# Mixture-of-experts stage of a two-layer encoder: steps of 512 inner columns, gathers for two experts at once, down products one step later

## What is computed

```
def _swiglu(h, w1, w3, w2):
    return (jax.nn.silu(h @ w1) * (h @ w3)) @ w2

def _moe(h, router, w1, w3, w2):                  # 8 experts, each token goes to 2
    ...
    top_val, top_idx = lax.top_k(logits, TOP_K)
    gates = jax.nn.softmax(top_val, axis=-1)
    gate_full = jnp.sum(one_hot(top_idx, N_EXPERTS) * gates[..., None], axis=1)
    for e in range(N_EXPERTS):
        out = out + gate_full[:, e:e + 1] * _swiglu(t, w1[e], w3[e], w2[e])
```

## Time and profile before

| | |
|---|---|
| median of 3 executions | 1885.35 us (1885.23 to 1887.1) |
| span of the profiled execution, first to last instruction | 1881.5 us |
| from that span to the median | 3.85 us; the profiled execution's own time is not listed apart from its span |
| PE matmul busy | 1803.4 us, 96% |
| DVE busy | 1344.3 us, 71% |
| ACT busy | 1025.5 us, 55% |
| moved by DMA | 470.67 MB, mean 250 GB/s |
| first up product of the mixture, last scatter | 822.8 us, 1862.6 us |

### The profile page before, as it was taken

The page is one execution under the profiler, slowest core; times in us unless marked ns, Lnnn a source line. Parts: engine busy times, 40 slices in busy tenths (PEclk is TensorE's granted clock), DMA queues, the critical chain, the costliest instruction groups (busy, mean ns, idle before and its releaser), DMA issues.

```text
span 1881.5 us, 31990 instructions
## 1 busy us (share of the span) xinstructions
PE 1803.4 (96%) x12801; PEld 1672.0 (89%) x12801; DVE 1344.3 (71%) x1265; ACT 1025.5 (55%) x1027; POOL 37.4 (2%) x73
## 2 busy tenths in 40 slices
PE   6999999999899999889999999999999999999996
PEld 6788998999788799889989999899899899898995
DVE  4555647444575466578888788888888888887886
ACT  4343443443334334356676667667676676666663
POOL 3000000000000000000000000000000000000000
PEclk9899999999898999979999999999999999999998
DMA  8342544655453345639999999999899999999993
GB/s 250 113 135 91 172 142 155 196 185 179 129 181 117 100 138 162 202 111 359 318 340 360 317 341 364 318 339 362 297 361 318 341 361 316 343 359 318 332 360 126
DMA packets 365521, 470.67 MB, mean 250 GB/s; under 512 B 9666, under 2 KB 331300, under 8 KB 365460
## 3 DMA queue, kind: packets, MB, share of 16 engines
q1 hardware_dynamic: 363124, 462.03, 73.4%
q0 software_dynamic: 2336, 7.78, 1.5%
HBM read 468.60 MB, written 1.06 MB: 250 GB/s over the span
## 4 chain that ended last, share of the span: by engine, by line
PE 86%; DVE 5%; DMA 3%; ACT 3%; issue 2%; SPq 1%; POOL 0%; DVEq 0%; ACTq 0%
PE PS L725 25%; PE PS L726 25%; PE PS L727 25%; DMA R1a_flat<-in_moe_w_dram 3%; PE PS L721 2%; DVE SPL L1613 2%; PE PS L1244 1%; PE PS L917 1%; ACT SPH L1339 1%; PE PS L1015 1%; PE PS L964 1%; PE PS L1003 1%; PE PS L935 0%; DVE st L1820 0%; PE PS L950 0%
## 5 line engine op out<-in xcount | busy, mean ns | idle before, releaser
L725 PE MATMUL PS<-SPH,XGH 128*128 128x256 f32 x1344 | 388.1, 289 | 1.6 <-issue 0.8
L727 PE MATMUL PS<-SPH,XGL 128*128 128x256 f32 x1344 | 381.0, 283 | 0.0
L726 PE MATMUL PS<-SPL,XGH 128*128 128x256 f32 x1344 | 381.0, 283 | 0.0
L1613 DVE TENSOR_TENSOR SPL<-RAW,SPH 128x2048 fp32r<-128x2048 f32 (+2 forms) x105 | 233.9, 2230 | 158.2 <-ACT SPH L1339 157.8
L725 PEld LDWEIGHTS PS<-SPH,XGH 128*128 128x128 f32 x1344 | 258.0, 192 | 8.9 <-issue 2.7
L726 PEld LDWEIGHTS PS<-SPL,XGH 128*128 128x128 f32 x1344 | 258.3, 192 | 5.7 <-issue 1.7
L727 PEld LDWEIGHTS PS<-SPH,XGL 128*128 128x128 f32 x1344 | 258.2, 192 | 0.0
L1339 ACT ACTIVATE SPH<-RAW 128x2048 fp32r<-128x2048 f32 (+2 forms) x105 | 195.4, 1864 | 86.5 <-PE PS L727 77.1
L725 PE MATMUL PS<-XTH,SPH 128*128 128x256 f32 x816 | 235.0, 288 | 2.7 <-DVE XTL L1613 1.4
L726 PE MATMUL PS<-XTL,SPH 128*128 128x256 f32 x816 | 233.0, 286 | 0.0
L727 PE MATMUL PS<-XTH,SPL 128*128 128x256 f32 x816 | 232.8, 285 | 0.0
(11 more groups left out here) (259 smaller groups left out, 4140.5 us busy)
## 6 DMA issues: line engine op xcount, KB each, us to landing
R1a_flat<-in_moe_w_dram SPq DMA_DIRECT2D x56, 1024.0 KB, 7.4
R3a_flat<-in_moe_w_dram SPq DMA_DIRECT2D x56, 1024.0 KB, 9.8
R1b_flat<-in_moe_w_dram SPq DMA_DIRECT2D x56, 1024.0 KB, 7.3
R3b<-in_moe_w_dram SPq DMA_DIRECT2D x56, 1024.0 KB, 9.7
R2a<-in_moe_w_dram SPq DMA_DIRECT2D x56, 1024.0 KB, 5.2
R2b<-in_moe_w_dram SPq DMA_DIRECT2D x56, 1024.0 KB, 5.2
RAW<-in_ffn_w_dram SPq DMA_DIRECT2D x33, 1024.0 KB, 5.2
RAW<-in_w_in_dram SPq DMA_DIRECT2D x28, 1024.0 KB, 5.2
```

Source lines behind the costliest of these rows:

```text
L725: mm(dst, wh, xh, start=start, stop=False)
L726: mm(dst, wh, xl, start=False, stop=False)
L727: return mm(dst, wl, xh, start=False, stop=stop)
L1613: return v.tensor_tensor(dst, src, hi, ALU.subtract)
```

## The change

- A step is a single pass over 512 columns. `up` now makes 128x512 outputs with 512-column products; place "a" and "b" are now the upper and the lower half of the 1024 rows of w1 and w3 (4 blocks each), so a call is 12 products of 512 columns. Silu, `hidden` and `take_turned` work on 512 columns once a step, and four transposes follow each other. The rows of w1 and w3 in HBM are 2 KB long in a transfer, which is still 1 MB.
- `down` of step k is run after the up products of step k+1, also from one expert to the next; the copies to YE and the scatter of expert n are run in the first two steps of expert n+1. Only the last expert has them behind it (`conclude`), where w2's parts go into the free buffers of w1.
- A gather makes 32 products of 256 columns for two experts, once in two experts.
- The low part of w2 has its own room, so that a w2 transfer waits for DVE's split and no longer for PE. The room is that of the attention tables (HK and others) for "b", and GB for "a". So POOL's load of the last gain and bias into GB now waits until all experts are added (`experts_added`), which DVE signals behind the If for further passes.
- The transfers are issued in the order w2a, w2b of step k, then w1a, w1b, w3a, w3b of step k+2.

The diff, cut to its core:

```diff
-    FE = 2 * P
-    STEPS = D_FF_E // (2 * FE)
+    FE = 4 * P
+    STEPS = D_FF_E // FE
+    PAIR = 2
+    GATHERS = N_EXPERTS // PAIR
...
-        S2L = {"a": over("S2al", [P, PIECE], F32R, "QK", PIECE)[:], "b": over("S2bl", [P, PIECE], F32R, "RAW", 0)[:]}
+        GBL = nc.alloc_sbuf_tensor_at("S2al", [P, PIECE], F32R, offset=gb_at)[:]
+        S2L = {"a": GBL, "b": over("S2bl", [P, PIECE], F32R, "HK")[:]}
...
# SP
+            def load2(c, e, k, j):
+                after(sp, lo2[c], k)
...
+                def step(j, following):
+                    load2("a", e, k0 + j, j)
+                    load2("b", e, k0 + j, j)
+                    if following:
+                        load1("a", following[0], k0 + j + 2, following[1])
+                        load1("b", following[0], k0 + j + 2, following[1])
+                        load3("a", following[0], k0 + j + 2, following[1])
+                        load3("b", following[0], k0 + j + 2, following[1])
...
# POOL
+                    if layer == DEPTH - 1 and i == 2:
+                        pool.wait_ge(experts_added, 1)
                     pool.dma_start(GB[:, 0, :], gg[layer].partition_broadcast(P)).then_inc(gb_loaded.sem, 16)
...
# PE
+                    for i, t in enumerate(ts):
+                        mm(dst, XGH[:, t, s], WH[:, i, :], start=(t == 0), stop=False)
+                        mm(dst, XGH[:, t, s], WL[:, i, :], start=False, stop=False)
+                    if fresh_lo is not None:
+                        pe.wait_ge(gather_lo, fresh_lo)
+                    for i, t in enumerate(ts):
+                        last = mm(dst, XGL[:, t, s], WH[:, i, :], start=False, stop=(t == KT - 1))
...
+                    k = k0 + 1
+                    up("a", 0, k, x)
+                    turn_hidden(k - 1)
+                    up("b", 0, k, x)
+                    if earlier:
+                        scatter(n - 1, 0)
+                        scatter(n - 1, 1)
+                        scatter(n - 1, 2)
+                    up("a", 1, k, x)
+                    up("b", 1, k, x)
+                    if earlier:
+                        scatter(n - 1, 3)
+                    down("a", k - 1, n, True, False)
+                    turn_gates(n, earlier)
+                    down("b", k - 1, n, True, False)
+                    def later(k, gather_of=None):
+                        up("a", 0, k, x)
+                        turn_hidden(k - 1)
+                        up("b", 0, k, x)
+                        up("a", 1, k, x)
+                        up("b", 1, k, x)
+                        if gather_of is not None:
+                            pe.wait_ge(gatedT_done, n + 1)
+                            gather(gather_of, 0, k + 1)
+                        down("a", k - 1, n, False, False)
+                        down("b", k - 1, n, False, False)
+                        if gather_of is not None:
+                            gather(gather_of, 1, k + 1)
...
# ACT
+                def period(k, earlier=True, ahead=True):
+                    if earlier:
+                        split2("a", k - 1)
+                        split2("b", k - 1)
+                        take_turned(k - 1)
+                    if ahead:
+                        split1("a", k + 1)
+                    silu(k)
+                    if ahead:
+                        split1("b", k + 1)
+                        split3("a", k + 1)
+                        split3("b", k + 1)
...
# DVE: as on ACT, with hidden(k) behind split1("b", k + 1); the first three
# of an expert's sums behind split1("a", k + 1) of the next one's second step
+                def conclude(n):
+                    k = n * STEPS + (STEPS - 1)
+                    split2("a", k, True)
+                    take_turned(k)
+                    split2("b", k, True)
+                    take_half(n)
+                    for i in range(4):
+                        add_rows(n, i)
...
                 extra_experts(dve, extra, listed[0])
+                dve.sem_inc(experts_added, 1)
```

More of the change, by code:

```diff
@@ L594, in _ @@
             layer_pieces(1)
[L596 to L624, removed]
@@ L1186, in down @@
[L1186 to L1191, removed]
+                    WH, WL = [w[c].rearrange("p (t n) -> p t n", t=KT // 2) for w in (WH, WL)]
+                    dst = PS[:, 2 + 2 * which, :]
+                    ts = range(KT // 2) if c == "a" else range(KT // 2, KT)
@@ L1204, in item, with scatter @@
[L1204 to L1227 removed]
+                def scatter(n, i):
+                    if i == 0:
+                        after(pe, y_act, n + 1)
+                        after(pe, y_dve, n + 1)
+                        pe.wait_ge(gatedT_done, n + 1)
+                    if i == 3:
+                        after(pe, scatter_done, n * 4 + 1)
+                    half, b = i // 2, i % 2
+                    mm(PS[:, SCATTER_BANKS[i], :], GATEDT[:, b * P:(b + 1) * P],
+                       YE[:, half * HALF:(half + 1) * HALF], start=True, stop=True).then_inc(scatter_ready, 1)
@@ L1249, in mixture, with pair @@
+                def pair(p, first=False, final=False, besides=None):
+                    expert(p * PAIR, 0, not first, p)
+                    expert(p * PAIR + 1, 1, True, None, None if final else p + 1, besides)
+                gather(0, 0, 0)
                 pe.wait_ge(rows_lo, 1)
-                gather(0, 1)
-                start(0)
-                with pe.Fori(0, N_EXPERTS - 1) as e:
-                    item(e, True)
+                gather(0, 1, 0)
+                pair(0, first=True)
@@ new lines, in gather, with silu @@
+                def gather(m, width=PAIR * P):
+                    for q, bank in enumerate(GATHER_BANKS):
+                        after(act, gather_ready, m * 8 + (q + 1))
+                        src = PS[:, bank, :].rearrange("p (t s) -> p t s", t=2)
+                        high(XGH[:, 2 * q:2 * q + 2, 0:width], src[:, :, 0:width]).then_inc(gather_hi, 1)
+                def silu(k):
+                    after(act, g_ready["b"], k + 1)
+                    after(act, hidden_done, k)
+                    a.activation(SIL, PS[:, 2, :], ACT.Silu).then_inc(silu_done, 1)
@@ L2113, in mixture, with pair @@
+                def pair(p, first=False, final=False, made=None, besides=None):
+                    e = p * PAIR
+                    expert(e, e, 0, not first,
+                           made=None if final else lambda: one_rows(p + 1, (e + PAIR, e + PAIR + 1), 0))
+                    expert(e + 1, e + 1, 0, True, not final, made, besides)
+                    if not final:
+                        gather(p + 1)
+                one_rows(0, (0, 1), 0)
                 dve.wait_ge(rows_hi, 1)
```

494 lines of the change are left out of this document (270 added, 224 removed).

## The result

The changed kernel takes 1831.8 us (median of 4 executions, 1827.22 to 1833.61), the kernel before in the same measurement 1885.29 us (1884.91 to 1887.1, 4 executions): ratio 0.9714, 95% interval 0.970 to 0.9728. The forecast was 1840.8 us, its range 1835 to 1855. The profiled execution took 1827.22 us, its span 1825.0.

The account below looks back on a forecast made before the run. PE's issue was taken as the bound. 56 x 16.90 + 7 x 4.0 + 11.5 + 6.2 = 992.1 us, 47.7 less; with the tail 44.6 less, span 1836.9, plus 3.85: 1840.8 us, range 1835 to 1855.

Parts of the forecast that it names:

- Up products, transposes, step: Each mixture step: 48 up products of 512 columns, transposes no gain; 17.42 becomes 16.90 us, 29.1 us over 56 steps.
- Gathers: Between experts: seven narrow gathers of 3.5 us become three wide ones of 3.84 us, saving 12.9 us.
- Boundaries: From one expert to the next, without the gather: 4.8 us become 4.0 for each of seven, saving 5.6 us.
- the slow product comes twice (0.8): In the next expert's second step: a scatter split in two places has a slow product behind each piece, 0.8 us.
- I keep 6.2: Mixture's slower first stretch, list of full experts and last half step's waits: 6.2 us before, taken as unchanged.
- The first gather: nothing, -1 to +1: Ahead of the mixture: twice the columns in as many instructions, costed at nothing, bounds -1 to +1 us.
- Tail: After the last expert: GB's transfers are now issued behind the If and land late, +3.1 us, bounds +0.9 to +6.7.
- its 2.88 us of issue: DVE's issue stretch near the end, ending at 1869.82, 3.5 us before GB's use; taken as it stood.
- 2.8 for the slow products, 2.2 for the landing and 1 at the start: Range's low end, 1835 us: no second slow product, GB's transfer landing fastest, first gather 1 us cheaper.
- The lead: In the steps: turned values, w2 and next splits are ready 5 us or more before PE wants them; waits cost nothing.
- Transfers: Each step needs a mean of 372 GB/s; with 2 KB rows at 397 its transfers take 15.5 us, hidden behind PE.
- rival (3): Strided 2 KB rows of w1 and w3 move badly; slower below 309 GB/s, 1966 us at 280; chance 0.02.

Follow-up runs that it names:

- single: The changed kernel with eight gathers of 128 columns, as in the kernel before, everything else kept: 1846.15 us, ratio 0.9801.
- before_no_if: The kernel before without reading the list of full experts and without the If for further passes on SP, PE, ACT and DVE: 1878.52 us.
- again: The changed kernel once more, unedited: 1830.31 us, ratio 0.9713 to the kernel before.
- gb_early: The changed kernel with GB loaded after the last but one step's down product, no longer behind the If: 1827.27 us, ratio 0.9698.
- dve_small: The changed kernel with DVE's small split of the turned values (0.69 us) done twice in each step: 1831.46 us in one execution.

## Why the prediction was right in kind and 9 us too high

By its own steps, all from the mark:

- **Up products, transposes, step.** 56 x 16.90 was forecast, 16.89 measured: 0.6 us less in all. Right. It is read from the starts; no run undoes the 512-column step by itself.
- **Gathers.** 3.84 was forecast, 3.83 measured. Right. The narrow ones, read at 3.5, cost 3.61 in single, which gives back 13.8 us for the 12.9.
- **Boundaries.** I took 4.0 us, and 3.68 was measured: 2.2 us over seven. The failed step is "the slow product comes twice (0.8)". Six of the eight records of the scatter take 1082.25 - 1080.08 = 2.17 us and the slow product behind them 0.63 for 0.23; the other two take 0.45 and theirs 0.64. 2.17 + 0.40 + 0.45 + 0.41 = 3.43, which is what one undivided scatter with one slow product costs in the earlier trace rows: 3.03 + 0.40. Its eight records start 0.43 us apart, and the product behind them is listed 0.03 us after the last one: its lateness is that last record's own time. A scatter is 8 x 0.43 us wherever it is cut, so dividing it is free; I had counted the 0.4 once for each piece.
- **"I keep 6.2."** What is left of the stretch is 986.65 - 56 x 16.89 - 7 x 3.68 - 3 x 3.83 = 3.6 us, 2.6 less. I did name the slower first stretch, and left it at its price; but it was a stretch at half clock, and the change moves the clock's return. Before, 18 of the first up products stood 0.213 us apart where 0.120 is usual, 1.7 us; after, none. The list of full experts, which I said would be hidden, accounts for at most the 0.7 us by which this stretch is shorter in before_no_if. The last few tenths are not accounted for.
- **"The first gather: nothing, -1 to +1."** The first up product comes 1.3 us earlier against the mark (1.5 at like clock there), though one more pair of one-hot rows makes the gather begin 0.4 us later. From the gather's start to the first up product it is 5.91 us after and 7.89 before; single, with the narrow gather, takes 6.85. So 0.9 us of the 2.0 are the clock. Most of the other 1.1 is the 0.83 us of "issue" ahead of the first up product, which stands in all four profiles of the kernel before and its edits and in none of the others; what removed it is not shown. A bound of 1 us on either side was made from instruction counts at one clock.
- **Tail.** +3.1 was forecast and +0.4 measured in the profiled execution, +1.3 in again. The wait for GB is there (2.45 and 3.34 us, gone in gb_early). The failed step is "its 2.88 us of issue" as a constant: 2.1 us of them went, for a reason that I can only narrow to the If and the place of the code. That part is luck: with the gap of dve_small the changed kernel would be near 1834, still just below the range.
- **Span to median.** The profiled execution of before was one of the faster ones by about 2 us, so the 3.85 us were no constant to add to a span. It doesn't matter in the difference, and the differences of the medians (53.5) and of the marks (54.0) agree.

2.2 + 0.6 + 2.6 + 1.3 + 2.7 = 9.4 us, of which the difference 54.0 - 44.6 is all. Each is small, and all have the same sign, which is how a range made from independent bounds was left. Its low end was built from "2.8 for the slow products, 2.2 for the landing and 1 at the start"; it had no term for the clock and none for stretches of issue that go, which are 2.6 us (1.7 + 0.9) and 2.9 us (2.1 + 0.8).

**The lead.** The argument that carried the sum, that all splits are 5 us ahead and DVE has a little time left, was right and careful: PE has no wait between 1000 and 1780 us, and a second split of 2.29 us in each step cost the mixture 3.1 us, nearly all at its edges. Its DVE sum of 15.1 us a step was 0.7 too high, as durations were added where starts should be.

**Transfers.** 372 GB/s was forecast and 374 is in the windows, 343 where a gather and an expert's end lengthen the steps. The price I worked out for 2 KB rows (397 GB/s) made no difference. In rival (3) the rate that fits 130.25 us is 307 GB/s, not 309; nothing rests on it. The Trainium skill (DMA: Bandwidth & Descriptors, Specifications) gives about 358 GB/s as HBM's limit for a core, and the same page says under Measured that a core that runs alone gets more, 425 GB/s for 16 MB. The trace agrees with the second: 374 over 100 us and 418 over 2 us. My text weighed only the first, which changed nothing in the sum.

## What to carry to other kernels

When the steady part of a kernel is bound by issue, count starts, not durations, and the sum over steps comes out within 1 us here; what then decides the error is the edges, where the clock, a jump and a wait are each worth microseconds. Look at the granted clock ahead of the stretch that you change: wider products right after a gap brought full clock back 7 us earlier here, which was worth 2.9 us. Before you lay a difference on an edit, look whether an idle stretch elsewhere moved too: 2.2 of the 2.3 us of dve_small were such a stretch. And compare two executions from a common mark just ahead of the change, since untouched code in front of it moved by 7 us, more than most of the terms.

## What the chip showed that I had not expected

- A scatter of four plain float32 products costs 3.43 us, 0.86 a product, with its slow follower, in one piece or in two.
- A passed If on DVE cost 2.9 us in one kernel and 3.3 with one instruction more behind it; in the changed kernel it is 0.7, and 3.0 with one operation more in each step.
- With 32 gather products of 256 columns full clock was back 4.5 to 4.8 us after the first of them, with 32 of 128 columns 11.7 to 11.9 us.
- Rows of 1 KB and of 2 KB kept the same step, with 366 and 374 GB/s over the same 100 us.
- With w2's transfers stalled behind PE, ACT waited for DMA 86 times for 116 us (R2a and R2b together), and the kernel lost 13.8: waits of an engine that has lead say little of the time.
